# Six landing buffers beside six split buffers in an expert loop

## The reference, cut to what matters

```
gp = softmax(t @ w_group + b_group);  g_idx = top_k(gl, 1)
top_v, top_i = top_k(el_sel, 2);      w2 = softmax(top_v) * p_g
for e in range(16):
    hid = silu(t @ w_gate[e]) * (t @ w_up[e])
    out = out + combine[:, e:e + 1] * (hid @ w_down[e])
```

## Time and profile before

| | |
|---|---|
| median of 3 runs | 1234.8 us (1227.67 to 1235.64) |
| profiled execution, first to last instruction | 1234.3 us (no other time of it is given) |
| instructions | 17374 |
| PE, DVE, ACT, POOL busy | 83%, 58%, 45%, 39% |
| mean granted TensorE clock | 0.915 of full |
| expert loop, first product of tile 0 to last write | 802 to 1195 us |

### The profile page before, as it was taken

The page is one execution under the profiler, slowest core; times in us unless marked ns, Lnnn a source line. Parts: engine busy times, 40 slices in busy tenths (PEclk is TensorE's granted clock), DMA queues, the critical chain, the costliest instruction groups (busy, mean ns, idle before and its releaser), DMA issues.

```text
span 1234.3 us, 17374 instructions
## 1 busy us (share of the span) xinstructions
PE 1025.4 (83%) x6261; PEld 911.5 (74%) x6261; DVE 713.3 (58%) x803; ACT 553.5 (45%) x677; POOL 482.8 (39%) x229
## 2 busy tenths in 40 slices
PE   2969899989989968899999887197889887988660
PEld 2959789978979957899999887176667666766540
DVE  3564558748848845212111114667788788788738
ACT  6542614615534533432332344236565565565523
POOL 3432404212412313334443322227465565555534
PEclk9978999999999989899999995599999899999795
DMA  9211312212312201223335436059898898888734
GB/s 310 63 41 35 91 35 78 74 34 77 84 39 77 68 17 35 68 85 85 85 85 161 135 94 240 18 186 341 279 383 309 300 345 313 318 322 310 265 135 183
DMA packets 152283, 191.38 MB, mean 155 GB/s; under 512 B 12358, under 2 KB 99676, under 8 KB 152248
## 3 DMA queue, kind: packets, MB, share of 16 engines
q1 hardware_dynamic: 145144, 165.79, 40.4%
q0 software_dynamic: 4656, 16.21, 3.9%
q10 hardware_dynamic: 2448, 8.91, 1.8%
HBM read 171.14 MB, written 19.75 MB: 155 GB/s over the span
## 4 chain that ended last, share of the span: by engine, by line
PE 50%; DVE 24%; issue 13%; ACT 7%; DMA 4%; ACTq 1%; DVEq 1%; POOL 0%; SPq 0%; POOLq 0%
PE PJ L420 38%; DVE MEM_R L1760 9%; DVE MEM L1579 2%; ACT MEM_R L1034 2%; PE MS L1257 1%; DMA CHUNK<-in_w_gate_dram 1%; PE NM L1237 1%; PE MS L1219 1%; DVE MEM_R L1878 1%; PE NM L1373 1%; PE PJ L1195 1%; PE PJ L1284 1%; PE MS L1264 1%; PE MS L1232 1%; DMA CHUNK<-in_w_up_dram 1%
## 5 line engine op out<-in xcount | busy, mean ns | idle before, releaser
L420 PE MATMUL PJ<-MEM_R 128*128 128x272 f32 (+2 forms) x5256 | 824.8, 318 | 39.7 <-DVE MEM_R L1878 8.9
L420 PEld LDWEIGHTS PJ<-MEM_R 128*128 128x128 f32 x5256 | 753.2, 193 | 101.4 <-issue 18.2
L638 POOL TENSOR_TENSOR MEM_R<-RAW,MEM_R 128x1024 fp32r<-128x1024 f32 x82 | 207.5, 2538 | 403.8 <-ACT MEM_R L790 403.8
L1760 DVE TENSOR_TENSOR MEM_R<-CHUNK,MEM_R 128x2048 fp32r<-128x2048 f32 x67 | 244.4, 3665 | 48.3 <-ACT MEM_R L1034 48.3
L726 POOL TENSOR_TENSOR MEM_R<-CHUNK,MEM_R 128x2048 fp32r<-128x2048 f32 x33 | 161.3, 4888 | 159.6 <-ACT MEM_R L1034 159.6
L1034 ACT CAST MEM_R<-CHUNK 128x2048 fp32r<-128x2048 f32 x100 | 188.2, 1908 | 30.7 <-DMA CHUNK<-in_w_gate_dram 19.4
L790 ACT CAST MEM_R<-RAW 128x1024 fp32r<-128x1024 f32 x82 | 85.3, 1049 | 118.8 <-DMA RAW<-in_w_pb_dram 41.2
L1719 DVE TENSOR_TENSOR MERGED<-PJ,MEM 128x544 f32<-128x544 f32 x16 | 11.6, 724 | 148.9 <-PE PJ L420 148.9
L1579 DVE SCALAR_TENSOR_TENSOR MEM<-MEM 128x548 f32<-128x548 f32 x72 | 66.8, 928 | 8.5 <-DVE MEM L1579 0.5
L1087 ACT CAST MEM_R<-NM 128x512 fp32r<-128x512 f32 x17 | 10.0, 586 | 100.4 <-DVE MEM L1885 100.4
L1409 PE MATMUL MS<-MEM 128*128 128x128 f32 x136 | 23.9, 334 | 32.5 <-DMA MEM<-t_rows,MEM 32.5
(11 more groups left out here) (287 smaller groups left out, 999.3 us busy)
## 6 DMA issues: line engine op xcount, KB each, us to landing
CHUNK<-in_w_up_dram SPq DMA_DIRECT2D x34, 1024.0 KB, 8.3
CHUNK<-in_w_down_dram SPq DMA_DIRECT2D x34, 1024.0 KB, 5.5
CHUNK<-in_w_gate_dram SPq DMA_DIRECT2D x32, 1024.0 KB, 6.3
RAW<-in_w_in_dram SPq DMA_DIRECT2D x58, 512.0 KB, 3.7
expert_rows<-MEM ACTq DMA_DIRECT2D x17, 512.0 KB, 7.0
expert_rows<-MEM SPq DMA_DIRECT2D x8, 512.0 KB, 5.1
RAW<-in_w_pa_dram SPq DMA_DIRECT2D x8, 512.0 KB, 3.7
RAW<-in_w_pb_dram SPq DMA_DIRECT2D x8, 512.0 KB, 3.7
```

Source lines behind the costliest of these rows:

```text
L420: ins = pe.matmul(out, w(a), x(b), start=first and n == 0, stop=last and n == 2)
L638: tt(lo, raw[slot], hi.bitcast(F32), ALU.subtract).then_inc(lo_done, 1)
L1760: tt(moe_hl[c][1], landed_at[c], moe_hl[c][0].bitcast(F32), ALU.subtract).then_inc(chunk_lo[c], 1)
```

## The change

- Every chunk gets a landing buffer (`raw_at`, CHUNK0 to CHUNK5) apart from its pair of high and low parts (`split_at`). EARLY and the chunk numbers 6 and 7 are gone, and the small tensors of the loop move to other places.
- SP loads chunk c of the next tile after `chunk_lo[c]` (the subtraction) in place of `chunk_used[c]`. In the loop it waits for `chunk_lo[0]` to `chunk_lo[5]` in this order, each with the value i + 1, and loads the chunk of tile i + 1 after each wait. Chunks 2 to 5 of tile 0 are loaded during `w_out`.
- ACT's `high_chunk(c, i)` waits for `chunk_used[c]`, since it now writes into a place that PE may still read. Chunks 4 and 5 of tile 0 are split after `route_ready`, 2 and 3 during the logits.
- DVE does all six subtractions of a tile; POOL does none of them and keeps the gathers.
- ACT copies the whole result of `down` (128 x 1024) by itself. `gs` is gone (its product is written over `sg`).
- The order of ACT's and DVE's calls in the loop is new.

The diff, cut to its core (the allocations are told above):

```diff
-        chunk_at = [cuts["mb"] + m * 2 * CH for m in range(2)] + [cuts["w"] + m * 2 * CH for m in range(4)]
-        assert chunk_at[5] + 2 * CH <= chunk_at[0]
+        raw_at = [cuts["mb"] + c * CH for c in range(6)]
+        split_at = [cuts["w"] + c * 2 * CH for c in range(4)] + [raw_at[5] + CH + m * 2 * CH for m in range(2)]
+        rows_at, tail_at = split_at[3] + 2 * CH - cuts["w"], split_at[5] + 2 * CH - cuts["w"]
+        assert cuts["w"] + rows_at + 2 * KT * P + F <= raw_at[0] and cuts["w"] + tail_at + F <= cuts["ident"]
...
                     for m in range(2):
                         chunk(m, 0)
+                if c > 3:
+                    chunk(c - 2, 0)
...
-            sp.wait_ge(mix_full, 4 * NCT2 + NCT2)
-            for c in range(2, 6):
-                chunk(c, 0)
-            for c in range(2):
-                sp.wait_ge(chunk_in[c], 16)
-                chunk(c, 1, dst=moe_early[c])
+            for c in range(6):
+                sp.wait_ge(chunk_lo[c], 1)
+                chunk(c, 1)
             sp.wait_ge(route_ready, 1)
             last = sp.value_load(last_i[0:1, 0:1], min_val=NE - 1, max_val=TILES - 1)
-            def next_step(i, first=0):
-                e_next = sp.value_load(te_i[0:1, ds(i + 1, 1)], min_val=0, max_val=NE - 1)
-                for c in range(first, 4):
-                    await_step(sp, chunk_used[c], i + 1)
-                    chunk(c, e_next)
-            next_step(0, first=2)
             with sp.Fori(1, TILES) as i:
                 with sp.If(i < last):
-                    next_step(i)
-                    e_now = sp.value_load(te_i[0:1, ds(i, 1)], min_val=0, max_val=NE - 1)
-                    for c in (4, 5):
-                        await_step(sp, chunk_used[c], i)
-                        chunk(c, e_now)
-            e_last = sp.value_load(te_i[0:1, ds(last, 1)], min_val=0, max_val=NE - 1)
-            for c in (6, 7):
-                await_step(sp, chunk_used[c - 6], last + 1)
-                chunk(c, e_last)
+                    e_next = sp.value_load(te_i[0:1, ds(i + 1, 1)], min_val=0, max_val=NE - 1)
+                    for c in range(6):
+                        await_step(sp, chunk_lo[c], i + 1)
+                        chunk(c, e_next)
...
-            low_chunk(1, 0)
-            low_chunk(4, 0)
...
-                act.wait_ge(chunk_in[c], i * 16 + 16 if c < 6 else 16)
-                early = c < 2 and isinstance(i, int) and i == 1
-                if early:
-                    act.wait_ge(chunk_used[c], 1)
-                act.copy(moe_hl[c][0], (moe_early if early else moe_raw)[c]).then_inc(chunk_hi[c], 1)
+                act.wait_ge(chunk_in[c], i * 16 + 16)
+                if not (isinstance(i, int) and i == 0):
+                    act.wait_ge(chunk_used[c], i)
+                act.copy(moe_hl[c][0], moe_raw[c]).then_inc(chunk_hi[c], 1)
...
-            def result(i, used):
-                act.wait_ge(used, i if used is chunk_used[5] else 1)
+            def result(i):
+                act.wait_ge(chunk_used[5], i)
                 await_step(act, y_out, i * 16)
-                act.copy(yt[:, 0:512], PJ[:, 2, :]).then_inc(y0_ready, 1)
-                act.wait_ge(y0_ready, i)
-                act.wait_ge(y1_ready, i)
+                act.copy(yt, PJ[:, 2:4, :].rearrange("p a n -> p (a n)")).then_inc(y_ready, 1)
+                act.wait_ge(y_ready, i)
...
             turned_rows(1)
+            high_chunk(0, 1)
             gate(0)
-            next_step(0)
+            high_chunk(1, 1)
+            high_chunk(2, 1)
+            turned_rows(2)
+            high_chunk(3, 1)
             turned_hidden(0)
             with act.Fori(1, TILES) as i:
                 with act.If(i < last):
+                    high_chunk(0, i + 1)
                     gate(i)
-                    next_step(i)
-                    result(i, chunk_used[5])
+                    high_chunk(1, i + 1)
+                    high_chunk(2, i + 1)
+                    turned_rows(i + 2)
+                    high_chunk(3, i + 1)
+                    high_chunk(4, i)
+                    result(i)
                     turned_hidden(i)
-                    high_chunk(4, i)
                     high_chunk(5, i)
             gate(last)
-            high_chunk(6, last)
-            high_chunk(7, last)
-            result(last, chunk_used[5])
+            high_chunk(4, last)
+            result(last)
             turned_hidden(last)
-            result(last + 1, chunk_used[7])
+            high_chunk(5, last)
+            result(last + 1)
...
-            low_chunk(0, 0)
+                dve.wait_ge(chunk_hi[c], i + 1)
+                tt(moe_hl[c][1], moe_raw[c], moe_hl[c][0].bitcast(F32), ALU.subtract).then_inc(chunk_lo[c], 1)
+            for c in range(4):
+                low_chunk(c, 0)
...
+            low_chunk(4, 0)
+            low_chunk(5, 0)
             rest_of_rows(1)
-            low_chunk(2, 0)
-            low_chunk(3, 0)
+            low_chunk(0, 1)
             gate(0)
-            low_chunk(0, 1)
+            low_chunk(1, 1)
+            low_chunk(2, 1)
             hidden(0)
             rest_of_rows(2)
-            low_chunk(2, 1)
             low_chunk(3, 1)
             rest_of_hidden(0)
-            low_chunk(5, 0)
             with dve.Fori(1, TILES) as i:
                 with dve.If(i < last):
+                    low_chunk(0, i + 1)
                     gate(i)
-                    low_chunk(0, i + 1)
+                    low_chunk(1, i + 1)
+                    low_chunk(2, i + 1)
                     hidden(i)
                     rest_of_rows(i + 2)
-                    low_chunk(2, i + 1)
                     low_chunk(3, i + 1)
-                    second_half(i, chunk_used[5])
+                    low_chunk(4, i)
                     rest_of_hidden(i)
                     low_chunk(5, i)
             gate(last)
             hidden(last)
-            low_chunk(7, last)
-            second_half(last, chunk_used[5])
+            low_chunk(4, last)
             rest_of_hidden(last)
-            second_half(last + 1, chunk_used[7])
+            low_chunk(5, last)
```

More of the change, by code:

```diff
@@ L321, in hawk_mlstm_hmoe_kernel @@
         ids = small(TAB).bitcast(U32)
[L323 to L329, removed]
+        xg = at("v1", D)
+        xgT = parts("w", KT, P, plus=rows_at)
+        hid = at("w", F, plus=rows_at + 2 * KT * P)
+        sg = at("w", F, plus=tail_at)
+        hidT = parts("xh", FT, P, plus=J * D)
+        yt = at("sig", D)
+        idcur = at("small", 2, plus=60).bitcast(U32)
+        assert cuts["v1"] + D <= cuts["cols"] and cuts["sig"] + D <= cuts["counts"]
         ya, yb = at("w", J, D), at("w", J, D, plus=J * D)
@@ L364, in hawk_mlstm_hmoe_kernel @@
         chunk_in, chunk_hi, chunk_lo, chunk_used = (
-            [sem(f"chunk_{what}{c}") for c in range(8)] for what in ("in", "hi", "lo", "used"))
+            [sem(f"chunk_{what}{c}") for c in range(6)] for what in ("in", "hi", "lo", "used"))
         xg_in, xT_full, xT_hi, xgT_ready = sem("xg_in"), sem("xT_full"), sem("xT_hi"), sem("xgT_ready")
@@ L511, in _, with chunk @@
             head_loads(H - 1, False)
-            def chunk(c, e, dst=None):
-                w, half = (w_gate, w_up, w_down, w_down)[c // 2], c % 2
+            def chunk(c, e):
+                w, half = (w_gate, w_up, w_down)[c // 2], c % 2
                 k = w.shape[2] // P // 2
                 src = w[0, ds(e, 1), half * k * P:(half + 1) * k * P, :].rearrange("a (k p) n -> p (a k) n", p=P)
-                sp.dma_start(moe_raw[c] if dst is None else dst, src).then_inc(chunk_in[c], 16)
+                sp.dma_start(moe_raw[c], src).then_inc(chunk_in[c], 16)
             mix_src = (win[:, :, C_A:C_A + D], win[:, :, C_B:C_B + D], wpa, wpb)
@@ L717, in _ @@
                 pool.dma_start(t_dram[tok(j), :], T[0:rows_of[j], j, :]).then_inc(t_out, 16)
-            def low_chunk(c, i):
-                if c < 6:
-                    await_step(pool, chunk_hi[c], i + 1)
-                else:
-                    pool.wait_ge(chunk_hi[c], 1)
-                landed_at = moe_early if c < 2 and isinstance(i, int) and i == 1 else moe_raw
-                tt(moe_hl[c][1], landed_at[c], moe_hl[c][0].bitcast(F32), ALU.subtract).then_inc(chunk_lo[c], 1)
             def gather(col):
@@ L1045, in _ @@
                              (MS, PJ)[j % 2][:, half, :].rearrange("p (m n) -> p m n", m=4)[:, :, 0:n]).then_inc(tT_ready, 1)
-            high_chunk(2, 0)
-            high_chunk(3, 0)
+                if 1 <= j <= 2:
+                    high_chunk(j + 1, 0)
             act.wait_ge(gaps_ready, 1)
@@ L1424, in gate_up, with down @@
                     last.then_inc(chunk_used[c], 1)
-            def down(i, chunks=(4, 5)):
+            def down(i):
                 pe.wait_ge(hidT_ready, i)
-                for c in chunks:
-                    pe.wait_ge(chunk_lo[c], i if c < 6 else 1)
+                for c in (4, 5):
```

(14 more changed lines are left out.)

35 lines of the change are left out of this document (8 added, 27 removed).

## The result

| | before | after |
|---|---|---|
| median | 1234.8 us (1227.67 to 1235.64) | 1307.9 us (1303.56 to 1309.0) |
| ratio to before | | 1.060, 95% interval 1.057 to 1.063 |
| span of the profiled execution | 1234.3 us | 1301.8 us |
| mean granted TensorE clock | 0.915 | 0.89 |

The change makes the kernel 6.0% slower. The forecast was 1293 us, with 1262 to 1330 as its range.

What follows compares the result with a forecast made beforehand. Bound: the expert loop's chain of waits (late loads, DVE and POOL taking turns, late gathers), 4.6 us a pass. Sum: 1234.3 - 4.3 before the loop + 60.8 in it + 1.6 behind = 1292.4, so 1293 us; range 1262 to 1330.

Steps and rivals of the forecast that it cites:

- The step that decides: Expert loop: SP's in-order waits hold chunks 0 to 3 behind chunk 5, so loads come in one burst; 28.0 us a pass.
- The walk of a pass: Expert loop, timed from DVE's end of chunk 5 to its next: 28.2 us, or 26.5 with the gather outside the burst.
- The first passes: Start of the expert loop: first pass 18.6 us with loads issued in time, second 26 us on meeting the burst.
- Subtractions on DVE alone: Expert loop: DVE needs 16.6 us per tile, below PE's 18.6, and taking turns with POOL is gone.
- Before the loop: Router's small steps: five additions fall from 5.36 to 1.0 us without POOL's subtraction, so some 4.3 us go.
- The sum: Whole kernel: 1234.3 - 4.3 + 60.8 + 1.6 = 1292.4 us of span, so a median of 1293 us, 4.7% slower.
- Behind the loop: Tile 16's products to the result copy, with chunk 5's split: 29.2 us against 27.6 before, +1.6.
- Loads in time after all: Rival, expert loop: SP's order does not hold loads back, passes of 21 us, 1197 us in all; chance 5%.
- the transfers' sum: Expert loop, loads in time: six chunks at 2.66, gather 1.7, write 4.0, 21.7 us in sum, taken as 21.
- The slow clock: Rival, expert loop: PE's idling keeps its clock at 1.2 GHz, 34 us a pass, 1371 us; chance 5%.
- A slower burst: Rival, expert loop: five queued loads each take a tenth more, about 1.1 us a pass, 1308 us; chance 6%.
- A rule against the trace: Chunk loads: the skill's 358 GB/s gives 2.93 us a chunk, some 15 us more; the trace's 421 GB/s disagrees.

Runs made afterwards that it cites:

- second experiment: Changed kernel with SP's loop turned (chunks 4, 5, then 0 to 3), same order of waits, register loads now ahead of chunk 4: 1299.7 us, ratio 1.053.
- first experiment: Changed kernel with SP taking its waits in DVE's order, chunks 0 to 3 for tile i + 2, then 4 and 5: 1154.5 us, ratio 0.937.
- third experiment: Changed kernel with SP's waits in DVE's order, except that chunk 0 alone stays behind chunk 5: 1304.0 us, ratio 1.058.

## Why the prediction was right, point by point

**The step that decides.** It held. SP's wait for chunk 5 stands ahead of the loads of chunks 0 to 3, and undoing that order alone takes 153 us away. The walk of a pass gave 28.2 us with the gather in the burst, and I took 28.0; the 13 full passes have a mean of 28.16. That it fits to 0.2 us is luck: its parts differ and cancel. ACT starts on chunk 0 8.5 us after DVE's end, not 7.7; about 0.4 of that is SP's register loads between chunks 5 and 0 (second experiment; I had counted on chunk 5's transfer to cover them), the rest stays open. Chunk 2 comes 15.0 us after DVE's end in the mean of the 13 passes (15.9 in the one shown above), for which I had 14.7. Against that, from there to DVE's next end it takes 13.2 us and not 13.5, since operations in a row overlap by 0.1 us each. PE's idle time ahead of the hidden transposes is 6.5 to 8.7 us in these passes, where I had 9.

**The reading of the strips.** I wrote that no compute engine is busy throughout. PE was busy for 82% of the time from 790 to 1195 us, more than the DMA engines' share of 0.79. Nothing in the sum hangs on it.

**The first passes.** From product to product, as the sum has it, the first pass took 17.8 us for 18.6 and the second 28.0 for 26 (813.55, 831.38, 859.43).

**Subtractions on DVE alone.** Right that they cost less than the shared ones: 2285 ns each, and 48 us when they are moved in the kernel before. The subtractions are as short in the changed kernel, so I take that gain to be inside the 1308 us too, hidden by the stall.

**Before the loop.** The five additions are at 1.0 us (4.3 gone, as forecast):

```profile
771.74 1.02 DVE L1763 TENSOR_TENSOR MEM<-MEM 128x16 f32<-128x16 f32 x5
```

Tile 1's first product comes 6.0 us earlier than in the earlier trace rows (813.55 for 819.53). The other 1.7 lie ahead of the additions (771.74 for 773.48): the logits begin 1.4 us later than before, but take 3.1 less, and the granted clock in this execution was 0.70 from 738 to 760 us, for 0.55 before. I had not forecast either.

**The sum, term by term.** Ahead of tile 1: forecast -4.3, measured -6.0. From tile 1 to tile 16: forecast +60.8 (408.6 for 347.8), measured 1230.83 - 813.55 = 417.3, +69.5. Of these 8.7 us, 1.3 are the first two passes together, 2.1 the 13 others, and 5.3 the empty passes, which I had counted in the kernel before (the earlier trace rows has them as 5.77 of "issue") and left out of the sum after. That is the term that was mis-sized. Behind the loop:

```profile
1230.83 18.59 PE L415 MATMUL PJ<-MEM_R 128*128 128x512 f32 x72 [5.29 <-issue]
...
1252.56 8.59 PE L415 MATMUL PJ<-MEM_R 128*128 128x512 f32 x24 [2.70 <-DVE MEM_R L1855]
```

```profile
1261.35 1.01 ACT L1031 COPY MEM<-PJ 128x1024 f32<-128x1024 f32 x1 [7.82 <-PE PJ L415]
```

From 1230.83 to 1262.36 are 31.5 us for the 29.2 forecast. The terms of that forecast add up to 29.9, so 0.7 is a slip in the sum. The last products are the rest: DVE's last subtraction ends at 1255.9, and the products behind it take until 1261.2, 5.3 us for the 2.9 forecast, with a granted clock of 0.50 from 1252.5 to 1256.0 and of 0.75 after. From there to the end nothing changed (39.4 us in both). Behind the loop it was 27.6 us before, so in sum 1234.3 - 6.0 + 69.5 + 4.0 = 1301.8, against 1292.4. The rest of the 15 us to the median is that the profiled execution is the fastest of the four runs (1303.56 of 1307.9) and 1.8 us longer than its span, of which the forecast had 0.5.

**The rivals.** "Loads in time after all" did not happen, and its price was wrong too: with the order mended a pass takes 17.8 us, not 21, and the kernel 1154.5 us, not 1197. The false part is the transfers' sum. I priced the write at 4.0 us of the engines from the stretch 890 to 895 us, as if the write filled it. It doesn't:

```profile
891.61 3.11 SPq L520 DMA_DIRECT2D CHUNK<-in_w_gate_dram  x2
891.95 0.34 ACTq L1071 DMA_DIRECT2D expert_rows<-MEM  x1
```

Two loads are issued in it as well, and the engines stand still until 892. The page after has the writes of ACT's queue by themselves (packets, MB, share of 16 engines):

```profile
q10 hardware_dynamic: 2448, 8.91, 1.7%
```

8.91 MB are the 17 writes, and 1.7% of 1301.8 us is 22 us, so 1.3 us of the 16 engines for a write, not 4.0. With the chunks at the 421 GB/s of the earlier trace rows (2.5 us each, not 2.66) the sum is 15.0 + 1.7 + 1.3 = 18.0 us, for the 17.8 measured. In the first experiment all of a pass, 7.3 MB with write and gather, goes in that time. The slow clock did not set the pass: PE ran its 48 products in 12.2 to 13.6 us in the full passes, and it isn't on the chain; behind the loop it cost the 2.4 us above. A slower burst: single chunks still land 2.6 us apart (960.48 to 963.10), so no, although the median came out at that rival's 1308 us.

**A rule against the trace.** The Trainium skill, "DMA: Bandwidth & Descriptors", has loads from HBM limited to about 358 GB/s for a core. The first experiment reads 6 chunks and 128 rows in a pass, 6.8 MB in 17.8 us, which is 383 GB/s, and writes 0.5 MB besides; in all the trace has 414 GB/s. By the rule the reads alone would take 19.0 us (an estimate from the page's figure). So the trace disagrees here too, over twelve passes and not only in a stretch of 5 us.

**What stays open.** Why chunk 0 takes 6.5 us from its issue in the burst when the shortest takes 4.7: chunks 4 and 5 ahead of it would explain it by the sum of their transfers, and the third experiment agrees (more chunks ahead, later still), but it wasn't tried with chunk 4 alone out of the way. The mended pass is bound by PE: from 850 to 1080 us of the first experiment PE has no idle time and no engine waits for a load. How much room the transfers have left beside it was not tried; with a share of 1.04 it can't be much.

## What to carry to other kernels

A prefetch is as early as the wait ahead of it in its queue. When a transfer is moved to an earlier condition, write down for one pass the order in which the issuing engine waits and the order in which the conditions come true; any wait that comes true last and stands in the middle turns everything behind it into a burst. An engine that is only a queue of waits shows no busy time, so ask the trace for its waits. And two parts of one change can have opposite signs: here the split of work was worth 48 us alone and the loads 153 in the wrong order, so test the parts before the whole is dropped.

## What was not expected of the hardware

- The DMA engines and TensorE were both full for twelve passes of 17.8 us, at 414 GB/s and a granted clock of 1.00; in the kernel before the passes were at 289 to 350 GB/s.
- The write of 512 KB takes 1.3 us of the 16 engines, and moving it out of the way of the loads changed nothing (1305.4 and 1307.9 us). A price read from the share of a stretch of 5 us, with a pause and two loads in it, had been three times that.
- Seven empty passes of a loop in five streams cost some 3.5 to 6.5 us in one kernel and some 8 in another, while no engine's record shows work; taking them away gave it back.
- Two register loads on SP with the turn of its loop put 1.8 us between two issues that otherwise follow each other in 0.6 to 0.7 us.
